# Twenty modulation products in attention: one accumulator row pair each, summed in two groups

## The chip, the cores and the metric

The kernel runs on one core of one Trainium2 chip. The metric is the device time of one execution in microseconds. The kernel before took 1193.83 us, the median of three runs (1192.38 to 1194.75).

## The reference, cut to what matters

Two layers act on 256 latent tokens and 256 context tokens of width 1024. Each layer has an attention part and a mixture-of-experts part, and both are modulated: shifts, scales and gates come from two conditioning vectors, `c` and `c_ctx`.

```
silu_c, silu_cc = silu(c), silu(c_ctx)
for l in range(2):
    sh1, sc1, g1, sh2, sc2, g2 = split(silu_c  @ ada_w[l] + ada_b[l], 6)   # ada_w[l]: 1024 x 6144
    (the same with silu_cc for the context tokens)
    h = rms(x) * (1 + sc1) + sh1
    y = attention(h, hc)                 # 16 query heads, 8 global and 8 local (window 128, with a sink)
    x = x + g1 * (y @ w_out[l])
    h = rms(x) * (1 + sc2) + sh2
    x = x + g2 * grouped_moe(h)          # 16 experts, the best 2 of each token
```

The modulation vectors are a product of a 2 x 1024 matrix with 2 x 6144 columns of weights, 50 MB in all. This case is about where these products are gathered.

## The kernel before, in words

Each engine has its own program, written out by hand in the order in which it runs, and semaphores tie the programs together. Everything is float32, so every TensorE product is issued as two passes, and a count of matmuls in the profile is twice the count of `mm` calls, except for transposes.

**Modulation units.** The 12288 columns of `ada_w` are cut into 24 units of 512 columns (2 MB each). `ada_unit` (lines 349 to 367) multiplies one unit on TensorE: `scv`, 128 x 2 per k-block, is the stationary operand and the 512 weight columns are moving. Eight k-blocks go to four column groups of the array, k and k + 4 to the same one, so that the result lies in bank 7 as four partial sums, at rows 32q and 32q + 1. ScalarE copies the whole bank to `parts` in `h_t` (`ada_parts`, line 763), TensorE transposes it in four blocks of 128 x 128 into bank 2 or 7 (`ada_turn`, line 376), and VectorE adds the four partial sums into `mods` (`ada_sum`, line 963). A unit may write bank 7 only when the sum of the unit before it is done (line 360). Units 0 to 3 run before layer 0's projections. Units 4 to 23 run inside layer 0's attention.

**Attention** (TensorE from line 437, ScalarE from 765, VectorE from 994). Layer 0 has 64 steps, one for each query head and tile of 128 tokens, called heads here. Heads 0 to 31 have 512 keys and heads 32 to 63 have 256. Of each 16 heads the last eight are local; those of the first 32 have a mask product added (line 467). TensorE works in iterations of two heads n and n + 1: the scores of both (464, 467), the transposes of the probabilities of heads n - 3 and n - 2 (476), in every second iteration the value products of four heads (493), and last a modulation unit, if one is due. A unit is due where a head number is 1 modulo 3, its `ada_turn` where it is 0 modulo 3, between the two transposes; so of three iterations two have a unit and one has none. VectorE does for head n the row maximum (1006, 1008 or 1011), then for head n - 1 the reciprocal and the scaling of the probabilities (1020, 1021). ScalarE does the exponential of head n (777, 778) and copies the transposed probabilities of head n - 2 (789), then `ada_parts` where n is 1 modulo 3.

**The weight loads.** SP issues the loads (`load_ada`, line 263) in one queue. In attention four slots of `ring` hold the units; a slot is loaded again when the unit that used it has signalled `ada_used`. Behind unit 23's load stand the two halves of `w_out`, gated by units 20 and 21, and behind them expert weights, gated by unit 23, by the end of attention and by the end of the output projection. Loads 5 to 7 are issued when the projections are done and two small transfers of swapped keys have landed.

**After attention** come the output projection (line 523), the norm, the routing and a loop over experts, all on TensorE's path. The expert weights are loaded slot by slot as the loop frees them.

Of the kernel before, what the change touches and what calls it, by code (L numbers as in the profile page):

```python
# [49 lines left out]
MAX_CHUNKS = [n * NE + 2 * t * P // CHUNK for n, t in zip(LEAST, TOK_TILES)]  # L50
ROWS = P * -(-CHUNK * (max(MAX_CHUNKS) + 1) // P)
GT = max(MAX_CHUNKS) + 2

C_ID, C_BLK, C_SWP = 0, P, 2 * P
# [52 lines left out]
def backbone(nc, x, c, ctx_in, c_ctx, ada_w, ada_b, attn_norm_g, ffn_norm_g, w_in, qn_global, kn_global,  # L108
             qn_local, kn_local, sink_logit, w_out, router_w, router_b, w_gate, w_up, w_down, table, out):
    with ExitStack() as stack:  # L110
# [3 lines left out]
        def sem(name):  # L114
            return stack.enter_context(nc.semaphore(name))
# [50 lines left out]
        rope_b = probs[:, 1, 0:SEQ]  # L166
        probs_t = h_t[:, 0:4, :]
        parts = h_t[:, 5, :]
        y_t = tokm[:, :, :].rearrange("p t n -> p (t n)").rearrange("p (k n) -> p k n", k=KD)
        smx = h_t[:, 4, 0:64]  # L170
        negmax = h_t[:, 4, 64:128]
# [48 lines left out]
        yg_in = [[sem(f"yg_in{l}_{t}") for t in range(4)] for l in range(DEPTH)]  # L220
        y_scaled, y_summed, c_turned, xc_ready = sem("y_scaled"), sem("y_summed"), sem("c_turned"), sem("xc_ready")
        o_turned, o_act, o_dve, out_done = sem("o_turned"), sem("o_act"), sem("o_dve"), sem("out_done")
        dve_step = sem("dve_step")

        def ada_bank(u):

            return bank[2 if u < 4 else 7]

        def units(l):

# [115 lines left out]
        def _(pe):  # L346
# [3 lines left out]
            def ada_unit(u):  # L350

                if u < 4:
                    s = (6, 0, 1, 2)[u]
                    pe.wait_ge(ada_in[u], 16)
                else:
                    s = (6, 3, 4, 5)[u % 4]
                    pe.wait_ge(ada2_in[u % 4], 16 * (u // 4))
                if u > 3:
                    pe.wait_ge(ada_summed, u)  # L360
                elif u > 0:
                    pe.wait_ge(parts_ready, u)
                w = ring[:, s, :].rearrange("p (k n) -> p k n", k=KD)
                for k in range(KD):
                    q = k % 4
                    last = mm(bank[7][32 * q:32 * q + 2, :], scv[:, k, :], w[:, k, :],  # L366
                              start=(k < 4), stop=(k >= 4))
                last.then_inc(ada_used, 1)

            def ada_turn(u):  # L370

                pe.wait_ge(parts_ready, u + 1)
                if 0 < u < 4:
                    pe.wait_ge(ada_summed, u)
                for m in range(4):
                    last = turn(ada_bank(u)[:, P * m:P * m + P], parts[:, P * m:P * m + P], ident)
                last.then_inc(ada_turned, 1)

            def first_sums():
# [58 lines left out]
            def attention(l):  # L438
                ub, gb = sum(UNITS[:l]), sum(UNITS[:l]) // 4
                us = units(l)  # L440

                def scores(n):
                    tt, T = us[n][0:2]
                    k0, kn = keys(tt)
                    if n == 0:
                        pe.wait_ge(qk_done, 10 * (l + 1))
                        pe.wait_ge(swapped, 64 * (l + 1))
                    if n >= 4:
                        pe.wait_ge(exp_done, ub + n - 2)

                    parts, masked = [(0, kn)], None
                    if T == 1 and tt < 2:
                        masked = (P, 2 * P) if tt == 0 else (0, P)
                        parts = [(0, P), (2 * P, kn), masked] if tt == 0 else [(P, kn), masked]
                    pair = []
                    for i in (n, n + 1):
                        kv, r = us[i][2:4]
                        a = r % 2
                        rows = slice(HD * a, HD * a + HD)
                        pair.append(((qk_t[:, T] if a == kv else sq[T])[rows, k0:k0 + kn],  # L460
                                     qk_t[rows, 2 + 4 * T + 2 * kv + r // 2, P * tt:P * tt + P], bank[i % 4]))
                    for c0, c1 in parts:
                        for k_t, q_t, o in pair:
                            last = mm(o[:, c0:c1], q_t, k_t[:, c0:c1], start=True, stop=(c0, c1) != masked)  # L464
                    if masked:
                        for k_t, q_t, o in pair:
                            last = mm(o[:, masked[0]:masked[1]], ident, band[tt], start=False, stop=True)
                    last.then_inc(sc_done, 2)

                def turn_probs(n):  # L470
                    tt = us[n][0]
                    pe.wait_ge(p_scaled, ub + n + 1)
                    if n >= 2:
                        pe.wait_ge(pt_ready, ub + n - 1)
                    for q in range(keys(tt)[1] // P):
                        last = turn(bank[4 + n % 2][:, P * q:P * q + P], probs[:, n % 4, P * q:P * q + P], ident)  # L476
                    last.then_inc(p_turned, 1)

                def values(g):

                    tt, T, kv, _ = us[4 * g]
                    k0, kn = keys(tt)
                    pe.wait_ge(pt_ready, ub + 4 * g + 4)
                    if g == 0:
                        pe.wait_ge(v_ready, 2 * (l + 1))
                    if g >= 1:
                        pe.wait_ge(y_evac, gb + g)
                    nk = kn // P
                    col = P * T + HD * kv  # L490
                    for q in range(nk):
                        for odd in range(2):
                            last = mm(bank[6][HD * odd:HD * odd + HD, 0:256],  # L493
                                      v_tok[:, k0 // P + q, col:col + HD],
                                      probs_t[:, q, 256 * odd:256 * odd + 256], start=(q == 0), stop=(q == nk - 1))
                    last.then_inc(pv_done, 1)

                for n in range(0, UNITS[l] + 4, 2):
                    if n < UNITS[l]:
                        scores(n)  # L500
                    if 3 <= n < UNITS[l] + 3:
                        turn_probs(n - 3)
                    for i in (n, n + 1):
                        if l == 0 and i % 3 == 0 and 0 < i <= 60:
                            ada_turn(3 + i // 3)
                    if 2 <= n < UNITS[l] + 2:
                        turn_probs(n - 2)
                    if n >= 6 and n % 4 == 2:
                        values(n // 4 - 1)
                    for i in (n, n + 1):  # L510
                        if l == 0 and i % 3 == 1 and i < 60:
                            ada_unit(4 + i // 3)
# [180 lines left out]
        def _(act):  # L693
# [62 lines left out]
                    do(v_tok[:, 2 * q:2 * q + 2, :].rearrange("p t n -> p (t n)"), bank[5 + q][:, :],  # L756
                       ACT.Identity).then_inc(v_ready, 1)

            def ada_parts(u):
                act.wait_ge(ada_used, u + 1)  # L760
                if u > 0:
                    act.wait_ge(ada_turned, u)
                do(parts, bank[7][:, :], ACT.Identity).then_inc(parts_ready, 1)

            def attention(l):
# [26 lines left out]
                for n in range(UNITS[l] + 2):  # L792
                    if n < UNITS[l]:
                        exponentials(n)
                    if n >= 2:
                        probs_out(n - 2)
                    if l == 0 and n % 3 == 1 and n // 3 < 20:
                        ada_parts(4 + n // 3)

            def route(l):  # L800
                nt = TOK_TILES[l]
# [138 lines left out]
        def _(dve):  # L940
# [3 lines left out]
            def link(ins):  # L944

                chain[0] += 1
                ins.then_inc(dve_step, 1)
                dve.wait_ge(dve_step, chain[0])
# [7 lines left out]
                    gv = vec[:, g0:g0 + KD].unsqueeze(2).to_broadcast([P, KD, 2])  # L956
                    link(v.tensor_tensor(gain[:, l, w], gain[:, l, w], gv, ALU.mult))

            def ada_sum(u):

                dve.wait_ge(ada_turned, u + 1)
                ps = ada_bank(u)[:, :].rearrange("p (m q x) -> p m x q", m=4, q=4)[:, :, 0:2, :]
                v.tensor_reduce(mods[:, 4 * u:4 * u + 4, :], ps, AX.X, ALU.add).then_inc(ada_summed, 1)

            def add_bias(m0, m1):
                dve.wait_ge(ada_summed, m1 // 4)
                bias = vec[:, V_ADAB + m0:V_ADAB + m1].unsqueeze(2).to_broadcast([P, m1 - m0, 2])
                link(v.tensor_tensor(mods[:, m0:m1, :], mods[:, m0:m1, :], bias, ALU.add))

# [25 lines left out]
            def attention(l):  # L995
# [2 lines left out]
                nu = UNITS[l]  # L998
                dve.wait_ge(v_mm, 2 * (l + 1))
                link(v.memset(esink[:, 0:nu], 0.0))  # L1000

                def maxima(n):
                    tt, T, kv, r = us[n]
# [27 lines left out]
                for n in range(nu + 4):  # L1031
                    if n < nu:
                        maxima(n)
                    if 1 <= n < nu + 1:
                        scale_probs(n - 1)
                    if n >= 7 and n % 4 == 3:
                        y_out(n // 4 - 1)
                    if l == 0 and n % 3 == 0 and 0 < n <= 60:
                        ada_sum(3 + n // 3)

            def add_attention(l):
                width = P * TOK_TILES[l]
# [246 lines left out]
```

## Time and profile before

| what | before |
|---|---|
| median of three runs | 1193.83 us |
| lowest and highest run | 1192.38 and 1194.75 us |
| span of the profiled execution | 1192.8 us |
| its engines: TensorE, weight loads, VectorE, ScalarE busy | 82%, 52%, 37%, 32% of the span |
| DMA, mean over the span | 254 GB/s |
| first score product of layer 0's attention | 147.96 us |
| first product of layer 0's output projection | 293.93 us |
| TensorE on the chain that ended last | 67% of the span |

The profiled execution is reported by its span, from its first to its last instruction; it has no time of its own beside that. The median of the runs is 1.0 us above this span, which is what lies around it.
### The profile page before, as it was taken

The numbers are of one execution on the slowest core, as the hardware profiler recorded it, in microseconds if no ns is written. First come the engines' busy times: TensorE is split into PE (matmuls) and PEld (weight loads), VectorE is DVE, ScalarE is ACT, GpSimd is POOL, SyncE is SP. The second block draws the span as 40 slices with busy tenths as digits, with TensorE's granted clock in tenths as the row PEclk, the third lists the DMA queues.
The fourth block names the chain that finished last, engine by engine and source line by source line (L and its number), as shares of the span: only waits on it lengthen the run. The fifth ranks groups of instructions, "written<-read, shape, count | busy, mean of one in ns | idle before, by whom it ended". The sixth has DMA issues, their size and how long they took to land.

```text
span 1192.8 us, 26429 instructions
## 1 busy us (share of the span) xinstructions
PE 980.8 (82%) x10601; PEld 623.3 (52%) x10602; DVE 435.6 (37%) x1194; ACT 380.8 (32%) x898; POOL 53.4 (4%) x96
## 2 busy tenths in 40 slices
PE   5699999888977999999999947998895855557982
PEld 2244654533437566767766625785584522324652
DVE  1356565666135222222222217568715200111222
ACT  3322265554014122222222224227703311322441
POOL 1000000000000000000000030000000000000001
PEclk9899999999995999999999977999996977877995
DMA  8993098798321089996989866005033899999933
GB/s 307 401 370 127 19 382 326 279 347 303 127 87 54 19 327 369 329 361 243 375 315 394 344 249 243 0 19 212 2 141 141 322 396 396 396 393 394 398 145 115
DMA packets 123776, 303.17 MB, mean 254 GB/s; under 512 B 5696, under 2 KB 5968, under 8 KB 123728
## 3 DMA queue, kind: packets, MB, share of 16 engines
q1 hardware_dynamic: 115872, 285.49, 64.2%
q0 software_dynamic: 6144, 16.79, 4.3%
q8 instruction: 33, 0.54, 0.2%
q10 hardware_dynamic: 1712, 0.23, 0.1%
q14 instruction: 15, 0.12, 0.0%
HBM read 290.95 MB, written 19.40 MB: 260 GB/s over the span
## 4 chain that ended last, share of the span: by engine, by line
PE 67%; SPq 10%; DVE 8%; DMA 7%; issue 4%; ACT 3%; ACTq 1%; POOL 1%; POOLq 0%; DVEq 0%
PE bank L577 17%; PE bank L423 10%; SPq L280 9%; PE bank L589 8%; PE bank L565 7%; PE bank L523 7%; PE bank L493 3%; PE bank L366 3%; PE bank L464 2%; DMA ring<-in_ada_w_dram 2%; DMA ring<-in_w_up_dram 2%; PE bank L476 2%; PE bank L534 1%; PE bank L432 1%; DVE h_t L1006 1%
## 5 line engine op out<-in xcount | busy, mean ns | idle before, releaser
L577 PE MATMUL bank<-ring,h_t 128*32 128x256 f32 x4160 | 257.0, 401 | 78.2 <-DMA ring<-in_w_up_dram 61.4
L577 PEld LDWEIGHTS bank<-ring,h_t 128*32 128x32 f32 x4160 | 162.7, 116 | 166.6 <-issue 108.4
L823 ACT COPY h_t<-bank 32x256 f32 x260 | 94.9, 365 | 223.6 <-PE bank L589 145.6
L1173 DVE TENSOR_TENSOR h_t<-h_t,bank 128x128 f32<-128x128 f32 x65 | 18.7, 288 | 324.9 <-ACT h_t L816 324.9
L589 PE MATMUL bank<-ring,h_t 128*32 128x256 f32 x2080 | 125.8, 380 | 7.7 <-issue 5.3
L423 PE MATMUL bank<-h_t,ring 128*128 128x512 f32 (+1 forms) x320 | 117.6, 522 | 12.3 <-ACT h_t L729 12.3
L565 PE MATMUL bank<-tokm,h_t 128*32 128x256 f32 x1760 | 111.3, 386 | 9.5 <-DVE h_t L1158 9.5
L589 PEld LDWEIGHTS bank<-ring,h_t 128*32 128x32 f32 x2080 | 77.8, 110 | 47.2 <-issue 17.8
L423 PEld LDWEIGHTS bank<-h_t,ring 128*128 128x128 f32 x320 | 62.4, 196 | 60.3 <-issue 40.9
L565 PEld LDWEIGHTS bank<-tokm,h_t 128*32 128x32 f32 x1760 | 67.9, 111 | 38.0 <-issue 11.2
L523 PE MATMUL bank<-tokm,ring 128*128 128x512 f32 (+1 forms) x256 | 83.1, 486 | 1.0 <-DVE tokm L1028 1.0
L816 ACT ACTIVATE h_t<-bank 128x128 f32<-128x128 f32 x65 | 18.1, 278 | 190.2 <-PE bank L577 190.2
L987 DVE RECIPROCAL work<-work 128x512 f32<-128x512 f32 (+1 forms) x20 | 54.3, 2713 | 58.7 <-ACT work L739 58.7
L1006 DVE TENSOR_REDUCE h_t<-bank 128x1 f32<-128x512 f32 (+1 forms) x96 | 57.4, 598 | 48.3 <-PE bank L464 26.9
L926 POOL DMA_DIRECT2D y_rows<-h_t x66 | 32.5, 493 | 888.3 <-ACT h_t L823 885.8
L789 ACT ACTIVATE h_t<-bank 128x512 f32<-128x512 f32 (+1 forms) x96 | 50.2, 524 | 57.3 <-PE bank L476 30.1
L523 PEld LDWEIGHTS bank<-tokm,ring 128*128 128x128 f32 x256 | 48.5, 190 | 35.7 <-issue 30.1
L778 ACT ACTIVATE ring<-bank,h_t 128x512 f32<-128x512 f32 (+1 forms) x96 | 58.6, 610 | 5.5 <-DVE h_t L1011 4.7
L476 PE MATMUL bank<-cst,ring 128*128 128x128 f32 x320 | 50.6, 280 | 8.0 <-DVE ring L1021 6.7
L1163 DVE STREAM_TRANSPOSE h_t<-bank 128x256 f32<-128x256 f32 x67 | 30.2, 450 | 53.4 <-PE bank L565 53.4
L476 PEld LDWEIGHTS bank<-cst,ring 128*128 128x128 f32 x320 | 35.3, 141 | 27.3 <-DVE ring L1021 19.6
L464 PE MATMUL bank<-ring 64*128 64x128 f32 (+3 forms) x144 | 47.0, 434 | 1.8 <-DMA work<-ring 1.8
(148 smaller groups left out, 994.9 us busy)
## 6 DMA issues: line engine op xcount, KB each, us to landing
ring<-in_w_gate_dram SPq DMA_DIRECT2D x32, 2048.0 KB, 12.7
ring<-in_w_up_dram SPq DMA_DIRECT2D x32, 2048.0 KB, 15.8
ring<-in_w_down_dram SPq DMA_DIRECT2D x32, 2048.0 KB, 16.4
ring<-in_ada_w_dram SPq DMA_DIRECT2D x24, 2048.0 KB, 11.0
ring<-in_w_in_dram SPq DMA_DIRECT2D x8, 1536.0 KB, 17.1
y_rows<-in_table_dram SPq DMA_DIRECT2D x1, 8704.0 KB, 45.7
y_rows<-h_t POOLq DMA_DIRECT2D x66, 128.0 KB, 5.2
ring<-in_w_out_dram SPq DMA_DIRECT2D x4, 2048.0 KB, 9.2
```

The costliest lines, as they stand in the source:

```text
L280: sp.dma_start(slot(s, k), src).then_inc(ew_in[l][s], 16)
L423: last = mm(bank[1 + i % 2][:, 0:widths[i]], qk_weights(i, k), h_t[:, k, 0:widths[i]], start=(k == 0), stop=(k == KD - 1))
L464: last = mm(o[:, c0:c1], q_t, k_t[:, c0:c1], start=True, stop=(c0, c1) != masked)
L476: last = turn(bank[4 + n % 2][:, P * q:P * q + P], probs[:, n % 4, P * q:P * q + P], ident)
L523: last = mm(bank[4 + m % 2][:, 0:P * nt], wout[k // 4][:, k % 4, P * m:P * m + P], y_t[:, k, 0:P * nt], start=(k == 0), stop=(k == KD - 1))
L565: last = mm(bank[5][CHUNK * q:CHUNK * q + CHUNK, 0:256], picks[:, tt, :], tokm[:, tt, 256 * q:256 * q + 256], start=(tt == 0), stop=(tt == ...
L577: last = mm(o.rearrange("r (s c i) -> r s c i", s=2, c=KF), hc_t[:, k, :], w[:, :, k, :, CHUNK * q:CHUNK * q + CHUNK], start=(k == 0), sto ...
L589: last = mm(bank[4][CHUNK * q:CHUNK * q + CHUNK, 0:256], he_t[:, k, :], wd[:, k, 256 * q:256 * q + 256], start=(k == 0), stop=(k == KF - 1))
L778: do(probs[:, n % 4, 0:kn], bank[n % 4][:, 0:kn], ACT.Exp, bias=negmax[:, n:n + 1], scale=SCALE, accum_out=lsum[:, n:n + 1]).then_inc(exp_ ...
L823: last = nc.scalar.copy(yrow[:, bass.ds(g % 2 * D + 256 * q, 256)], bank[4][CHUNK * q:CHUNK * q + CHUNK, 0:256])
L987: v.reciprocal(rstd[:, 0:n], rstd[:, 0:n])
L1006: link(v.tensor_reduce(smx[:, n:n + 1], bank[n % 4][:, 0:keys(tt)[1]], AX.X, ALU.max))
```

## The change: what it does

Units 4 to 23 are gathered in two groups, units 4 to 11 and 12 to 23. Each unit of a group adds into bank 7 at rows of its own: the stationary operand is now 32 columns wide, a window into `scv_wide` in which all but two columns are zero, and the place of the two columns is that of the unit within its group. The copy, the four transposes and the sum are made once for a group. They stand at head 22 (copy), 24 (transposes) and 25 (sum) for the first group, and at 58, 60 and 61 for the second. A unit waits for a sum only where it is the first of its group. `scv_wide` is set by a memset of 128 x 496 and a copy on VectorE at the start of layer 0's attention. Units 0 to 3 stay as they are.

```diff
+ADA_GROUPS = [(0, 1), (1, 2), (2, 3), (3, 4), (4, 12), (12, 24)]
+        scv_wide = h_t[:, 6, 0:496].rearrange("p (k c) -> p k c", k=KD)
             def ada_unit(u):
-                if u > 3:
-                    pe.wait_ge(ada_summed, u)
-                elif u > 0:
-                    pe.wait_ge(parts_ready, u)
+                n = [u0 <= u < u1 for u0, u1 in ADA_GROUPS].index(True)
+                u0, u1 = ADA_GROUPS[n]
+                if u == u0 and n > 3:
+                    pe.wait_ge(ada_summed, n)
+                    pe.wait_ge(scv_spaced, 1)
+                elif u == u0 and n > 0:
+                    pe.wait_ge(parts_ready, n)
...
+                        first_col = 30 - 2 * (u - u0)
+                        last = mm(bank[7][32 * q:32 * q + 32, :], scv_wide[:, k, first_col:first_col + 32], w[:, k, :],
+                                  start=(u == u0 and k < 4), stop=(u == u1 - 1 and k >= 4))
...
-                        if l == 0 and i % 3 == 0 and 0 < i <= 60:
-                            ada_turn(3 + i // 3)
+                        if l == 0 and i in (24, 60):
+                            ada_turn(4 if i == 24 else 5)
...
-                    if l == 0 and n % 3 == 1 and n // 3 < 20:
-                        ada_parts(4 + n // 3)
+                    if l == 0 and n in (22, 58):
+                        ada_parts(4 if n == 22 else 5)
...
+                ps = ada_bank(n)[:, :].rearrange("p (m q j x) -> p m j x q", m=4, q=4, x=2)
+                sums = mods[:, 4 * u0:4 * u1, :].rearrange("p (j m) x -> p m j x", m=4)
+                for m in range(4):
+                    last = v.tensor_reduce(sums[:, m], ps[:, m, 0:u1 - u0], AX.X, ALU.add)
+                last.then_inc(ada_summed, 1)
...
+                if l == 0:
+                    link(v.memset(scv_wide, 0.0))
+                    v.tensor_copy(scv_wide[:, :, 30:32], scv[:, :, :]).then_inc(scv_spaced, 1)
...
-                    if l == 0 and n % 3 == 0 and 0 < n <= 60:
-                        ada_sum(3 + n // 3)
+                    if l == 0 and n in (25, 61):
+                        ada_sum(4 if n == 25 else 5)
```

## Rows read from the trace of the kernel before

**Rows 1.** Windows by stretch: length, engines' busy time (count), granted clock, DMA share, GB/s.
```profile
157.76:229.97 72.21, 65.80 (x530) 37.14 (x532) 42.48 (x135) 41.52 (x105) 0.00 (x0) 1.00 0.91 333
229.97:284.55 54.58, 47.56 (x364) 21.44 (x366) 33.78 (x140) 30.27 (x102) 0.00 (x0) 1.00 0.85 310
284.55:293.93 9.38, 6.41 (x42) 3.31 (x42) 6.17 (x27) 6.26 (x23) 0.00 (x0) 1.00 0.89 324
804.60:868.60 64.00, 56.44 (x401) 35.29 (x401) 49.37 (x153) 45.59 (x114) 0.00 (x0) 0.97 0.26 99
```

**Rows 2.** Waits of TensorE from 157 to 285 us: total us, times, longest.
```profile
PE bank L376 <- ACT h_t L763: 9.7, 9, 1.2
PE bank L366 <- DVE mods L963: 2.2, 4, 0.7
```

**Rows 3.** Chain of waits in the heads with 512 keys: start, length, what.
```profile
162.10 1.83 PE bank L366 x16
...
166.61 0.60 ACT h_t L763
167.26 0.66 PE bank L376 x4
167.91 0.44 PE bank L476 x4
...
170.54 0.61 ACT h_t L789
171.19 1.95 PE bank L493 x16
...
174.97 1.08 PE bank L464 x12
176.04 0.66 PE bank L467 x4
...
190.81 1.06 PE bank L464 x4
```

**Rows 4.** The same chain in the heads with 256 keys.
```profile
245.59 0.22 PE bank L476 x2
245.81 1.01 PE bank L493 x8
246.83 0.63 PE bank L464 x4
...
287.91 0.34 DVE h_t L1006
...
289.14 0.34 DVE h_t L1006
```

**Rows 5.** The same chain in layer 1's attention, where VectorE sets the pace.
```profile
825.75 0.70 DVE h_t L1006
...
827.48 0.61 DVE h_t L1006
```

**Rows 6.** Groups by form, 157.76 to 229.97 us: busy us, mean ns, idle before.
```profile
L366 PEld LDWEIGHTS bank<-ring,scv 128*2 128x2 f32 x144 | 2.9, 83 | 9.7 <-issue 9.7
L963 DVE TENSOR_REDUCE mods<-bank 128x8 f32<-128x32 f32 x9 | 1.6, 183 | 0.0
```

**Rows 7.** Chain of waits in layer 0's expert loop: 64 passes of 256 columns.
```profile
484.03 3.45 PE bank L577 x64
```

**Rows 8.** Groups by form in that expert loop, 384 to 690 us.
```profile
L577 PEld LDWEIGHTS bank<-ring,h_t 128*32 128x32 f32 x2688 | 101.7, 110 | 58.6 <-issue 17.1 <-DVE h_t L1163 2.5
```

**Rows 9.** VectorE at the start of attention, in order of time.
```profile
146.29 0.11 DVE L1000 MEMSET h_t<- 128x64 f32 x1 [3.25 <-PE bank L432]
...
149.19 0.69 DVE L1006 TENSOR_REDUCE h_t<-bank 128x1 f32<-128x512 f32 x1 [2.79 <-PE bank L464]
```

**Rows 10.** Chain of waits: the first unit load that attention waits for.
```profile
147.90 7.86 DMA ring<-in_ada_w_dram
```

**Rows 11.** Window where the loads ran without a pause: columns as in Rows 1.
```profile
240.00:280.00 40.00, 34.88 (x267) 15.38 (x265) 25.40 (x107) 22.89 (x81) 0.00 (x0) 1.00 1.00 367
```

More of the change, by code:

```diff
@@ L222, in backbone, with ada_bank @@
         o_turned, o_act, o_dve, out_done = sem("o_turned"), sem("o_act"), sem("o_dve"), sem("out_done")
+        scv_spaced = sem("scv_spaced")
         dve_step = sem("dve_step")
-        def ada_bank(u):
-            return bank[2 if u < 4 else 7]
+        def ada_bank(n):
+            return bank[2 if n < 4 else 7]
         def units(l):
@@ L365, in ada_unit, with ada_turn @@
                     q = k % 4
-                    last = mm(bank[7][32 * q:32 * q + 2, :], scv[:, k, :], w[:, k, :],
-                              start=(k < 4), stop=(k >= 4))
+                    if u < 4:
+                        last = mm(bank[7][32 * q:32 * q + 2, :], scv[:, k, :], w[:, k, :],
+                                  start=(k < 4), stop=(k >= 4))
+                    else:
+                        first_col = 30 - 2 * (u - u0)
+                        last = mm(bank[7][32 * q:32 * q + 32, :], scv_wide[:, k, first_col:first_col + 32], w[:, k, :],
+                                  start=(u == u0 and k < 4), stop=(u == u1 - 1 and k >= 4))
                 last.then_inc(ada_used, 1)
[L370 to L374, printed above, removed]
+            def ada_turn(n):
+                pe.wait_ge(parts_ready, n + 1)
+                if 0 < n < 4:
+                    pe.wait_ge(ada_summed, n)
                 for m in range(4):
-                    last = turn(ada_bank(u)[:, P * m:P * m + P], parts[:, P * m:P * m + P], ident)
+                    last = turn(ada_bank(n)[:, P * m:P * m + P], parts[:, P * m:P * m + P], ident)
                 last.then_inc(ada_turned, 1)
@@ L757, in qkv, with ada_parts @@
                        ACT.Identity).then_inc(v_ready, 1)
[L759 to L762, printed above, removed]
+            def ada_parts(n):
+                act.wait_ge(ada_used, ADA_GROUPS[n][1])
+                if n > 0:
+                    act.wait_ge(ada_turned, n)
                 do(parts, bank[7][:, :], ACT.Identity).then_inc(parts_ready, 1)
@@ L957, in gains, with ada_sum @@
                     link(v.tensor_tensor(gain[:, l, w], gain[:, l, w], gv, ALU.mult))
[L959 to L963, printed above, removed]
+            def ada_sum(n):
+                dve.wait_ge(ada_turned, n + 1)
+                u0, u1 = ADA_GROUPS[n]
+                ps = ada_bank(n)[:, :].rearrange("p (m q j x) -> p m j x q", m=4, q=4, x=2)
[3 more added lines that the diff above has]
+                last.then_inc(ada_summed, 1)
             def add_bias(m0, m1):
-                dve.wait_ge(ada_summed, m1 // 4)
+                dve.wait_ge(ada_summed, 4 if m1 == 2 * KD else len(ADA_GROUPS))
                 bias = vec[:, V_ADAB + m0:V_ADAB + m1].unsqueeze(2).to_broadcast([P, m1 - m0, 2])
```

## The prediction

> **What bounds the kernel now.** I read the page's chain first: TensorE holds most of it, so a change counts if it shortens TensorE's way through its stage. The stage here is layer 0's attention. The windows by stretch cut it where units end: from the end of unit 5 to that of unit 14 (27 heads, nearly all with 512 keys), to that of unit 23 (27 heads, nearly all with 256 keys), and a tail to the output projection [rows 1]. TensorE is busy 91% of the first and 87% of the second stretch, VectorE 59% and 62%, ScalarE 57% and 55%. So TensorE is near its bound and the rest is short waits. The table of waits names them: nine times TensorE stands before `ada_turn` for the copy of bank 7, 9.7 us in all, and four times a unit stands for the sum of the one before, 2.2 us [rows 2]. The chain in order of time shows one case: the copy 0.60, then the four transposes 0.66, where 0.44 is the price of four transposes in flow [rows 3]. The copy is late because unit and `ada_turn` are only scores and one transpose apart, and ScalarE, in order, has put everything behind the copy.
>
> **What is removed.** 20 sets of copy, transposes and sum become 2. The set of unit 4 lay before unit 5's load had landed, and unit 23's stays as the second group's. Of the 18 between, unit 11's is replaced by the first group's, so 17 leave TensorE's path: 17 x 0.44 = 7.5 us of transposes [rows 3]. With them go the waits, 9.7 + 2.2 = 11.9 us [rows 2], and the slower start after a wait, 9 x (0.66 - 0.44) = 2.0 us. Ceiling: 21.4 us. The waits don't all go, because the heads have waits of their own which these have covered. I therefore build both stretches anew.
>
> **First stretch, 72.2 us now.** A pair of heads costs 1.06 without a mask, 1.08 + 0.66 = 1.74 with one, on average 0.70 a head; transposes 0.44 a head; value products 1.95 for four heads, 0.49 a head [rows 3]. That is 1.63 x 27 = 44.0 us, and nine units of 1.83 are 16.5: work of 60.5 us. New waits: value products wait for the copy of their last transposes, 0.61 with 0.44 of the next transposes beside it, so 0.2 seven times, 1.4 us. VectorE takes 1.73 for a masked head [rows 5], so two heads need 3.46; TensorE, in an iteration with neither unit nor values, comes back after 0.88 + 1.74 + 0.44 = 3.06. That happens once in 12 heads, 0.4 each, 0.9 us. Sum 62.8 us.
>
> **The switch of groups**, in the same stretch. Unit 12 now waits for the sum at VectorE's head 25, which stands behind two heads' work, not one: from the end of scores(24), 2 x 1.73, then the sum, then 0.14 to start, 4.2 us. TensorE has 3 x 0.44 = 1.3 to do until then, so it stands 2.9 us. Behind the waiting unit stand scores(26) and all the rest of TensorE; VectorE and ScalarE run dry behind them. With the group's transposes, 3.3 us. The four reductions take 32 elements in 183 ns now [rows 6], and 512 in 690 ns [rows 9]; 64 or 96 elements lie near the lower end, I take 0.2 each, 0.7 for four (0.7 to 2.8). First stretch: 66.1 us, a saving of 6.1.
>
> **Second stretch, 54.6 us now.** Scores 0.63 a pair, transposes 0.22 a head, values 1.01 for four [rows 4]: 0.79 x 27 = 21.3 us; nine units 16.5; the three heads of the larger size that reach into it 1.5. Work of 39.3 us. VectorE's pace is 1.24 a head [rows 4], 2.48 for two, against TensorE's 0.44 + 0.63 + 0.22 = 1.29: 1.2 once in 12 heads, 2.7 us. Waits before values I take at 0.35, seven times, 2.4 us. Sum 44.4 us, a saving of 10.2.
>
> **What is added.** (1) The memset and copy on VectorE. A memset of 64 columns took 0.11 us; 496 columns lie between that and 0.9 (8 times as much). VectorE is idle for 2.79 us just there, waiting for the first scores, which themselves wait for the swapped keys [rows 9]: nothing on the path; without that cover at most 1.0 us. (2) Stationary operands of 32 columns instead of 2. A load takes 110 ns in the expert loop against 83 [rows 6, 8]. The expert loop has the same shape of work: 64 passes of 256 columns on 32-column stationaries took 3.45 us, 54 ns a pass, so the loads lie beside the products and four passes run side by side [rows 7]. Sixteen passes of 512 columns at that rate are 1.72, against the 1.83 of a unit now. I charge only the first load of each unit, 20 x 0.027 = 0.5 us; bounds 0 and all 320 loads, 8.6 us. (3) In the tail VectorE is the chain [rows 4], and the second group's four reductions stand in it: 0.7 instead of 0.18, 0.5 us (bounds 0.5 and 2.6).
>
> Here a rule speaks against the change. The Trainium skill, "TensorE: Matmul & The Clock Gate", section "The mechanism" under Part 3, says that weight loads overlap running products only when the row group differs; here all products use all 128 rows. Rows 7 and 8 disagree: 64 loads of 110 ns are 7.0 us and the whole took 3.45. By the rule the sum would lose about 8 us; by the trace 0.5.
>
> **The loads' queue.** Each load is still freed by its own unit, so a faster loop asks earlier. A load of 2.1 MB at 367 GB/s takes 5.7 us [rows 11]; from issue to use the first took 7.9 [rows 10]. New pace: 7.3 us a unit in the first stretch, 4.9 in the second, so from unit 15 on the loads are slower than the loop and live on the lead of four slots. Unit 13 ends near 217, load 17 lands near 225, then each 5.7 later, load 23 near 259. Unit 23 starts near 267. The halves of `w_out` land near 265 and 271 and the projection starts near 279. Lead left: 7 us; the loads stay hidden. Unit 6 is tight as well: its load lands near 161.5 and it would now start at 161.6.
>
> **Sum.** 6.1 + 10.2 - 0.5 - 0.5 = 15.3 us. The gated expert loads (unit 23, end of attention, end of projection) all move with the stage, and the projection is 55 us of TensorE during which two pairs of them land, so I carry the whole 15.3 us through. The profiled span of 1192.8 becomes 1177.5; with the 1.0 us that lies around it, and from the median, 1178.5 us.
>
> **Rivals.**
> A. The heads' own latency takes the place of the removed waits. For: in layer 1, with no units at all, 32 heads take 64.0 us [rows 1] where TensorE's work is 1.63 x 32 = 52; a VectorE head costs 1.73. Against: a unit fills 1.83 us in two of three iterations. Then only the transposes go, 7.5, less the switch 2.9, less 1.0: 3.6, 1190.2 us.
> B. The loads run out. For: 100% DMA share from 240 to 280 already [rows 11]. Against: the lead of 7 us. If a load takes 6.7 beside denser traffic, the last units and `w_out` lose the lead and some 5 us: 1183.5 us.
> C. The weight loads of 32 columns are not hidden: 320 x 27 ns = 8.6 less the 0.5 charged, so 7.2 is left: 1186.6 us. This is what the Trainium skill's rule would give. Against it stand rows 7 and 8.
> D. Slower than before: the wide stationaries lose the running side by side of four column groups. A unit would be 16 passes of 213 ns (512 columns at the granted clock of 1.00), 3.4 us instead of 1.83, 20 times, +32 us: 1210 us. It decides from a pass rate of 155 ns on, where 15.3 us are used up. Rows 7 show 54 ns at 256 columns, so it would need a cause in the windows into `scv_wide` or in adding across units.
> E. It doesn't do what it says in time: the stage ends earlier, but the expert loop is bound by something that doesn't move. Against: every gate in SP's queue moves. 1193.8 us.
>
> **How the numbers follow.** Forecast 1173.5 to 1184, chance 0.60; A 0.15, B 0.10, C 0.05, D 0.05, E 0.05. What a measurement of this kernel tells from no change is about 0.2%, 2.4 us. Faster: the forecast, A, B, C, 0.90; same: E, 0.05; slower: D, 0.05. The range starts at 1173 (the ceiling of 21.4 us, less little) and reaches to 1189.5, into the better part of A, and leaves out D, E and the rest of A, about 0.2.
>
> **What would show it.** The four transposes appear six times in the trace, 24 instead of 96. The first stretch takes 66 us, the second 44, the tail 10, and the projection starts at 279 us. Before unit 12 TensorE waits some 3 us for the sum. A unit's chain piece stays near 1.85. The waits for `ada_turn` fall from 9.7 to about 2. In the second stretch new waits before transposes (for VectorE) and values (for ScalarE) appear, about 5 us. No unit waits for its load beyond unit 6. I am wrong if the second stretch stays above 50 us (A), if units wait for loads (B), if a unit's piece grows by 0.3 or more (C, D), or if the stage gains and the end doesn't (E).

## The result and the profile after

The changed kernel took 1228.1 us, the median of four runs (1218.3 to 1233.7), against 1194.3 for the kernel before beside it: a ratio of 1.0269, 95% interval 1.0210 to 1.0328. It is 34 us slower where 15 us faster were forecast, and its runs scatter over 15 us where those of the kernel before stay within 3.1. The profiled execution is the fastest of the four, with a span of 1216.4 us.

The windows of the changed kernel by stretch; the first three answer to the first three of [rows 1], the others are discussed below.

```profile
157.22:223.97 66.75, 62.37 (x499) 34.61 (x498) 41.55 (x131) 36.98 (x97) 0.00 (x0) 1.00 0.99 360
223.97:270.87 46.90, 43.59 (x329) 18.41 (x328) 31.69 (x131) 25.89 (x93) 0.00 (x0) 1.00 0.97 361
270.87:280.87 10.00, 6.54 (x43) 3.36 (x43) 6.74 (x30) 6.26 (x23) 0.00 (x0) 1.00 0.90 334
464.10:475.00 10.90, 1.25 (x13) 0.38 (x14) 0.97 (x3) 1.46 (x4) 0.49 (x1) 0.69 0.97 354
475.00:480.00 5.00, 5.00 (x64) 2.97 (x63) 0.00 (x0) 0.00 (x0) 0.00 (x0) 0.64 0.03 12
```

The stage did nearly what was forecast: 66.8 us (forecast 66.1), 46.9 (44.4) and 10.0 (9.9). The output projection starts at 280.87 us, 13.1 us earlier than before. So everything was lost, and 23.6 us more, behind the stage that the change touches. Four marks and the end place the loss:

| TensorE reaches | before | after | difference |
|---|---|---|---|
| output projection | 293.93 | 280.87 | -13.1 |
| layer 0's expert loop | 387.04 | 374.86 | -12.2 |
| layer 0's combine | 713.12 | 737.18 | +24.1 |
| layer 1's expert loop | 919.79 | 943.45 | +23.7 |
| end of the span | 1192.8 | 1216.4 | +23.6 |

All of it lies in layer 0's expert loop, 326.1 us before and 362.3 after, though its code and its work are the same. The chain of waits in that loop, first of the kernel before at its first jump back, then of the changed kernel at the same jump:

```profile
474.11 1.73 PE bank L589 x32
475.84 1.07 issue
476.91 3.66 PE bank L577 x64
```

```profile
462.39 1.73 PE bank L602 x32
464.12 6.99 issue
471.11 1.07 PE bank L590 x6
472.19 2.66 issue
474.84 5.23 PE bank L590 x57
```

"Issue" is idle time in which the engine waited for no other engine and no data transfer that the profile shows. It is 1.07 us in one and 6.99 + 2.66 in the other. The loop runs five times, so it has four jumps back, and the profiled execution has such a stop at three of them, at 464, 533 and 611 us. The granted clock falls to 0.50 during each stop and stays there for 3.7, 5.8 and 4.0 us behind it; that is the 0.64 in the window from 475 to 480, where 64 passes take 5.23 us instead of 3.66. The waits of TensorE in the loop and the page's row of the instruction queue, first of the kernel before, then of the changed one:

```profile
PE bank L577 <- issue: 10.3, 15, 1.1
q8 instruction: 33, 0.54, 0.2%
```

```profile
PE bank L590 <- issue: 36.0, 17, 7.3
q8 instruction: 60, 0.98, 0.3%
```

### The profile page after: what moved, and what is told of

Its sections match the earlier page's. It is cut to its first block, busy times and chain, and to the rows that moved or that the text cites. A ratio compares the mean times of both kernels' runs of the same rounds, so it can differ in the third digit from the quotient of the medians.

```text
span 1216.4 us, 26232 instructions
## 1 busy us (share of the span) xinstructions
PE 982.3 (81%) x10529; PEld 616.5 (51%) x10530; DVE 434.3 (36%) x1196; ACT 371.5 (31%) x880; POOL 53.2 (4%) x96
## 4 chain that ended last, share of the span: by engine, by line
PE 65%; SPq 10%; DVE 8%; DMA 7%; issue 6%; ACT 3%; ACTq 1%; POOL 1%; POOLq 0%; DVEq 0%
PE bank L590 17%; PE bank L436 9%; SPq L285 9%; PE bank L602 8%; PE bank L578 7%; PE bank L536 7%; PE bank L506 3%; PE bank L379 3%; DMA ring<-in_ada_w_dram 2%; PE bank L477 2%; DMA ring<-in_w_up_dram 2%; PE bank L489 2%; PE bank L547 1%; DVE h_t L1026 1%; PE bank L445 1%
## 5 line engine op out<-in xcount | busy, mean ns | idle before, releaser
L590 PE MATMUL bank<-ring,h_t 128*32 128x256 f32 x4160 | 269.1, 410 | 104.1 <-DMA ring<-in_w_up_dram 61.2
L590 PEld LDWEIGHTS bank<-ring,h_t 128*32 128x32 f32 x4160 | 165.6, 118 | 200.1 <-issue 142.5
L602 PE MATMUL bank<-ring,h_t 128*32 128x256 f32 x2080 | 129.9, 381 | 7.7 <-issue 5.3
L578 PE MATMUL bank<-tokm,h_t 128*32 128x256 f32 x1760 | 114.9, 386 | 9.5 <-DVE h_t L1178 9.5
L602 PEld LDWEIGHTS bank<-ring,h_t 128*32 128x32 f32 x2080 | 78.9, 110 | 48.0 <-issue 17.8
L489 PE MATMUL bank<-cst,ring 128*128 128x128 f32 x320 | 49.0, 281 | 11.8 <-DVE ring L1041 10.5
## 6 DMA issues: line engine op xcount, KB each, us to landing
ring<-in_w_gate_dram SPq DMA_DIRECT2D x32, 2048.0 KB, 12.8
ring<-in_ada_w_dram SPq DMA_DIRECT2D x24, 2048.0 KB, 12.9
y_rows<-in_table_dram SPq DMA_DIRECT2D x1, 8704.0 KB, 47.6
```

Of the source, the lines that this page charges most:

```text
L578: last = mm(bank[5][CHUNK * q:CHUNK * q + CHUNK, 0:256], picks[:, tt, :], tokm[:, tt, 256 * q:256 * q + 256], start=(tt == 0), stop=(tt == ...
L590: last = mm(o.rearrange("r (s c i) -> r s c i", s=2, c=KF), hc_t[:, k, :], w[:, :, k, :, CHUNK * q:CHUNK * q + CHUNK], start=(k == 0), sto ...
L602: last = mm(bank[4][CHUNK * q:CHUNK * q + CHUNK, 0:256], he_t[:, k, :], wd[:, k, 256 * q:256 * q + 256], start=(k == 0), stop=(k == KF - 1))
```

## The experiments

The fillers in all of them are waits on a semaphore that is already past its value, written in pairs; each pair is one instruction. In the changed kernel TensorE's first product starts at 12.8 us; 162 fillers at the start delay it to 18.8, and 81 hardly (13.0). They take about 0.11 us each, and until 12.8 us TensorE is idle in any case.

**1. The old place for the changed kernel.** 162 fillers.

```diff
+            for _ in range(324):
+                pe.wait_ge(down_mm[0], 1)
             pe.wait_ge(cst_in, 16)
```

> The changed kernel with 162 more instructions at the start of TensorE's program: waits that are already met, while TensorE stands idle for its first inputs. 162 is what the change took out of TensorE's program ahead of the expert loop, so the loop lies again where it lay before. Theory P (placement): layer 0's expert loop is TensorE's longest loop body, some 1600 instructions or 6.25 blocks of 16 KB, and whether it stays resident depends on where it starts within a block. Then the instruction queue shows about 33 packets again instead of 60, the three stops of 10 us at the jump back are gone, the loop takes 305 us instead of 341, and the attention's gain of 13 us stays: 1181 us. Theory D (dynamics: the loop starts earlier against its weight loads, or the wide stationaries leave something behind): still 1218 to 1233 us, 60 packets.

Measured: 1190.0 us (seven runs, 1188.4 to 1194.0), ratio 0.9951 (0.9938 to 0.9964). 33 packets, no stop above 1.1 us, loop 386.1 to 711.9. Everything of the change is still there; what differs is the place of the code, and a start that is later by 6.0 us. That counts against theory D, and experiments 3 and 4 settle it. The kernel is 38 us faster for 162 instructions that do nothing. It stays 9 us above the 1181 expected: the fillers held the start up by 6.0 us, which had not been counted, and by the output projection the delay against the changed kernel is 8.5 us (289.35 against 280.87).

**2. A new place, 81 fillers.** The same edit with 162 waits.

> The changed kernel with 81 instructions instead of 162. Theory P: the loop starts just over a block boundary, which is the best place it can have, 7 blocks; so fast as well, 1181 us, although no kernel so far had this place. Were it the old place itself that matters (what lies ahead of the loop, or the total length), 1218 us or more. Theory D: 1218 to 1233 us.

Measured: 1185.6 us (four runs, 1182.7 to 1187.8), ratio 0.9918 (0.9889 to 0.9948), 33 packets, 5 us above the 1181 expected. So it isn't the old place that counts but a class of places.

**3. One block later.** 256 fillers.

> The changed kernel with 256 more instructions, one block: the loop lies one whole block later and at the same place within it as in the changed kernel. Theory P: slow as the changed kernel, 1218 to 1233 us, about 60 packets. If more instructions ahead of the loop help by themselves, or the waits at the start change the timing, 1181 us.

Measured: 1243.9 us (1237.9 to 1251.3), ratio 1.0425 (1.0367 to 1.0484), 61 packets, three stops of 9.6 to 10.5 us. The start is held up by 16.4 us (first product at 29.2), about as much as the 15.8 us that the time lies above the changed kernel's. More instructions don't help, and a later start doesn't either; the place within a block decides.

**4. The kernel before, at the bad place.** 94 fillers in the kernel without the change.

> The kernel before, attention unchanged, with 94 instructions more at the start: its loop now lies at the place within a block where the changed kernel's lies. Theory P: the loop loses 25 to 50 us with nothing of the change in it, stops of about 10 us at the jump back, about 60 packets: 1230 to 1245 us. Theory D: 1194 us, since nothing is different but waits already met.

Measured: 1241.9 us (1235.0 to 1243.9), ratio 1.0381 (1.0337 to 1.0425). Its page and its chain:

```profile
q8 instruction: 70, 1.15, 0.4%
```

```profile
477.65 7.01 issue
...
485.73 2.65 issue
...
685.64 6.93 issue
```

This is the test from the other side: no part of the change is in this kernel, its attention is that of before (projection at 295.7), and it loses 46 us. It has the stop at all four jumps, where the profiled run of the changed kernel has it at three. The fillers of experiment 3 give the same place within a block and three stops, so the place doesn't fix the number; what does is open. That the changed kernel's other runs, up to 15 us slower, had the fourth stop too is not shown, as only one run is profiled.

**5. Fillers behind the loop.**

```diff
                 experts(l)
+                if l == 0:
+                    for _ in range(162):
+                        pe.wait_ge(down_mm[0], 1)
                 combine(l)
```

> The changed kernel with 81 fillers behind layer 0's expert loop, where TensorE waits for the gathered rows. The total length of TensorE's program and the place of everything behind are those of the version with 81 at the start, but the first loop lies where the changed kernel has it. Theory P: slow, 1218 to 1235 us, about 60 packets. If the total length or layer 1's place mattered: about 1186 us.

Measured: 1218.8 us (two runs, 1217.8 and 1219.8), ratio 1.0194, 60 packets, three stops. The time lies at the lower edge of the changed kernel's own, and 33 us above that of the same fillers at the start. The length of the program and the place of layer 1's code don't matter. Layer 1's loop (736 instructions) has its packets only in its first round, in the kernel before and in the changed one.

**6. and 7. Where the step lies.** 48 fillers (24 at the start, 12 each ahead of the waits for the routing mask and for the routing), and 24 fillers at the start.

> The changed kernel with 48 fillers ahead of layer 0's expert loop: 24 at the start and 12 each at the two waits of the routing, so that none of them is on TensorE's path. Theory P: what counts is whether the 1601 instructions of the loop touch 7 or 8 blocks of 256. The loaded program begins some instructions ahead of the one written; from the kernels so far that offset lies between 20 and 114. With 48 fillers the loop starts at 219 plus the offset, so it touches 7 blocks if the offset is 37 or more: then 33 packets, no stops, and as the fillers cost nothing 1181 to 1183 us. With an offset under 37, slow: about 1220 us.

> The changed kernel with 24 fillers at the start: the loop starts at 195 plus the offset. Theory P: fast (1183 us, 33 packets) if the offset is 61 or more, slow (1218 us or more, 60 packets) if it is less. Nothing between the two: it's a step and not a slope. If the time followed the number of fillers, it would lie between 1186 and 1218.

Measured: with 48, 1186.5 us (six runs, 1183.3 to 1188.5), ratio 0.9927 (0.9909 to 0.9946), 4 us above the 1181 to 1183 expected. With 24, 1242.2 us (two runs, 1241.2 and 1243.2), ratio 1.0395. Instruction queue and waits of the one with 48, then of the one with 24:

```profile
q8 instruction: 33, 0.54, 0.2%
PE bank L593 <- issue: 10.6, 15, 1.1
```

```profile
q8 instruction: 69, 1.13, 0.4%
PE bank L590 <- issue: 58.3, 15, 13.0
```

A step, as the theory says, between 24 and 48 fillers: the offset is 37 to 60 instructions. (The 114 in the first expectation above should be 84, since from 85 on the changed kernel's loop would touch seven blocks; nothing hangs on it.) Here all four stops are 12.9 to 13.0 us long, in one piece, and the kernel is slower than the changed one. The price of a stop thus depends on the place too.

**8. Place or size.** One token tile left out of the gathers of layer 0, and 48 fillers to keep the start.

```diff
-                    for tt in range(nt):
+                    used = nt - 1 if l == 0 else nt
+                    for tt in range(used):
```

> The changed kernel in which layer 0 gathers rows of three token tiles instead of four (the fourth tile's rows are left out), which takes 96 instructions out of the loop, and 48 fillers at the start, so that the loop starts exactly where the changed kernel's starts. Theory P: place and size count together. With 1505 instructions from the same start the loop touches 7 blocks instead of 8: no stops at the jump back, some 33 packets, though the start is the bad one. The work left out itself is worth some 30 us (0.43 us for each of 65 gathers). If the start's place alone counted: stops of 9.7 us as in the changed kernel.

Measured: 1164.0 us (two runs, 1162.3 and 1165.8), 32 packets, no stop above 1.1 us, the first jump included. The time can't be compared, since the kernel leaves work out; the stops and packets can. The loop starts where the changed kernel's starts and is 96 instructions shorter, which puts its end into the seventh block. So it isn't the start alone, nor how near to a block's end the jump lands: start and size count together, as the number of blocks touched would have it.

**9. and 10. What a stop costs.** Layer 0's expert weights loaded by half, then by a sixteenth.

```diff
+                    n = 4096 // k
+                    if l == 0:
+                        n = n // 2
-                    sp.dma_start(slot(s, k), src)...
+                    sp.dma_start(slot(s, k)[:, :, 0:n], src[:, :, 0:n])...
```

> The changed kernel with layer 0's expert weights loaded by half (half the columns of each slot; the rest of the slot holds older data, so layer 0's experts compute something else; the instructions, their order and places are the same). Theory P with its price: at each jump back TensorE waits for a block of instructions that stands behind the weight loads just issued, two of 2 MB, 10 us at 390 GB/s. With half the bytes the stops fall from some 9.7 us to about 5, the packets stay at about 60. If the price were a fixed cost of a jump to a block that isn't resident, the stops would stay near 9.7 us.

> The changed kernel with a sixteenth of layer 0's expert weights loaded (32 or 64 columns of each slot; the experts compute something else). With half the bytes the stops were 7.2 to 8.2 us instead of 9.7, so traffic is not the main price. If the rest is a fixed price of a block that isn't resident, the stops stay at 6 to 7.5 us with hardly any weight traffic. If it was still the queue ahead of the block, they fall under 3 us.

Measured stops at the four jumps, by half and by a sixteenth:

```profile
468.00 8.23 issue
...
536.12 8.11 issue
...
610.94 7.56 issue
...
669.90 7.23 issue
```

```profile
468.12 4.38 issue
...
531.29 4.94 issue
...
602.52 4.72 issue
...
660.05 4.88 issue
```

Neither theory had it. Against 9.7 us with full loads (mean of three, the two pieces added) the stops are 7.8 with half and 4.7 with a sixteenth, where DMA moved 33 GB/s from 500 to 560 us. So about 4.7 us are left with hardly any weight traffic, and 5 more come with it. Not in proportion: half the bytes take only 1.9 off. The time was 1216.3 and 1205.8 us (two runs each), both with 69 packets.

The starts of the instruction packets divide a stop further. With a sixteenth of the loads the first packet starts with the stop (468.0) and TensorE goes on 4.5 us later, though the packet itself takes 1.1. With full loads the first packet starts only 2.6 us after the stop began (466.7), and TensorE goes on 4.4 us behind its start, for 1.07 us; then it stands again, as the next block isn't there either: that packet starts 5.7 us after the first, against 3.2 with a sixteenth. With half the loads the first starts 3.6 us after the stop began and the second 3.3 later. So a stop holds two fetches one behind the other, and what weight traffic adds lies in the waits for their starts. With 24 fillers the first packet starts 2.8 us after the stop began, the second 6.1 later, and TensorE goes on only 4.1 behind the second, 12.9 in one piece. The counted place agrees: there the jump lands 1 to 24 instructions ahead of a block's end, in the changed kernel 25 to 48.

**11. The change with the place mended.** 35 fillers ahead of each of the two waits of layer 0's routing, none at the start.

> The changed kernel with 70 filler instructions (waits already met) ahead of layer 0's expert loop, 35 where TensorE waits for the routing mask and 35 where it waits for the routing, both times idle for 5 us or more. At 0.11 us each they cost nothing there. Theory P: the loop starts just past or at a block boundary, 33 packets, no long stops; the start of the kernel is not touched, so the whole 13 us of the attention stay: 1181 us against 1194. If the 1186 us of the version with 81 came from something other than its fillers at the start, 1184 to 1187.

Measured: 1186.1 us (six runs, 1183.7 to 1190.0), ratio 0.9927 (0.9906 to 0.9948). Its profiled execution keeps the stage's gain whole: projection at 281.20, loop at 376.56, combine at 702.79, end of the span at 1182.0 against 1192.8. Of the 12.7 us at the projection 10.8 arrive. The time is 5 us above the 1181 expected, as in the expectation's second case; one wait of TensorE shows the fillers themselves, which took longer than the idle time that was to hide them:

```profile
PE bank L566 <- issue: 2.8, 1, 2.8
```

**12. The sums one head earlier.**

```diff
-                    if l == 0 and n in (25, 61):
-                        ada_sum(4 if n == 25 else 5)
+                    if l == 0 and n in (24, 60):
+                        ada_sum(4 if n == 24 else 5)
```

> The same, and the sums of the two groups stand one head earlier on VectorE, at heads 24 and 60 instead of 25 and 61. TensorE stood 2.5 us before unit 12 for the sum. Theory: the sum is ready one head's work (1.6 us) earlier, TensorE stands about 0.9 us, and up to 1.6 us is gained: 1179.5 us. If the heads behind it make up for the wait in any case, equal to the version without it.

Measured: 1185.3 us (1182.7 to 1188.0), ratio 0.9910 (0.9891 to 0.9929). TensorE's wait before unit 12 fell from 2.52 to 0.89 us as expected. The stage takes 133.0 us from first scores to projection, against 133.6: part of the gain goes into other waits, and in the medians the two can't be told apart, where 1179.5 us had been expected. It has the lowest median of all kernels that do the whole work, by less than the measurement resolves.

## Why the prediction was wrong

**The stage, right.** The terms can be checked one by one in the changed kernel. The chain at the switch of groups:

```profile
202.81 0.44 PE bank L389 x4
203.24 0.44 PE bank L489 x4
203.68 2.52 issue
206.20 1.92 PE bank L379 x16
```

The wait was forecast at 2.9 and is 2.52. The waits of TensorE from 157 to 281 us, in the place of [rows 2]:

```profile
PE bank L489 <- DVE ring L1041: 5.0, 10, 0.8
PE bank L506 <- ACT h_t L802: 3.0, 11, 0.5
PE bank L379 <- issue: 2.5, 1, 2.5
```

The 11.9 us of waits are gone, and those of the heads' own are 8.0, as the argument had it. The second stretch came out 2.5 us longer than forecast, and not by its waits: they are 3.3 us there (2.0 for VectorE, 1.3 for ScalarE) where 5.1 were forecast. TensorE is busy for 43.6 us in it, and the sum had 39.3 of work. So the total came nearer than its terms, by luck. Row 2 of [rows 1] would have given the work: 47.6 us busy less nine sets of transposes at 0.44 are 43.6. No unit after unit 5 waits for its load. The memset and the copy on VectorE and the group's reductions:

```profile
146.10 0.47 DVE L1019 MEMSET h_t<- 128x496 f32 x1 [0.17 <-DVE h_t L1017]
146.61 0.18 DVE L1020 COPY h_t<-scv 128x16 f32<-128x16 f32 x1
148.70 0.69 DVE L1026 TENSOR_REDUCE h_t<-bank 128x1 f32<-128x512 f32 x1 [1.91 <-PE bank L477]
...
274.10 0.74 DVE L979 TENSOR_REDUCE mods<-bank 128x24 f32<-128x96 f32 x4
```

The memset (0.47, bounds 0.11 to 0.9) is hidden, with 1.91 us of idle time left; four reductions take 0.74 (forecast 0.7). A unit's piece on the chain is 1.85 to 1.92 with 32 columns against 1.83 to 1.90 with two, and its weight loads 109 ns each:

```profile
L379 PEld LDWEIGHTS bank<-ring,h_t 128*32 128x32 f32 x288 | 7.6, 109 | 18.5 <-issue 18.5
```

Rival C and the rule behind it fall: the loads are hidden. So does rival D; rivals A and B did not come about. D's price was too low as well: it took 213 ns for a pass of 512 columns that runs alone, but in the output projection before, where passes run one after another, 119 recorded ones take 51.34 us, 0.43 each, at a granted clock of 1.00.

**The step that failed** is in the sum: "all move with the stage, and the projection is 55 us of TensorE during which two pairs of them land, so I carry the whole 15.3 us through." The weight loads and their gates do move. What was not looked at is that the change also moves code. It takes 162 instructions out of TensorE's program ahead of its longest loop, and the loop's seven touched blocks become eight. The sum has no term for it, which puts it at nothing. It costs 36 us in the loop of the profiled execution, 25.7 of it more waiting; the other 10.5 fit the lower clock in and behind the stops, which was not taken apart further. Rival D gave the right sign and half the size (+16 us against +34) with a mechanism that isn't there, and E had the place and not the sign. The test for it stood in the trace of before: the row of the instruction queue with its 33 packets, none in the rounds after the first, said that the loop was resident, and the count of the program said that a shift of the loop by 162 instructions could make it touch one block more. (With the offset known since, it had room for 54 to 77 instructions one way and 114 to 137 the other.) What that costs, no row of before shows.

**What the change is worth** is 13.1 us at the end of its stage, and in the medians 8.9 us with the place mended (1195.0 to 1186.1). That is 6 us less than the 15.3 forecast: above the forecast's 1184, and inside the wider range that reaches to 1189.5. 1.9 us are lost in that kernel's trace between the projection and the end, with fillers that outlast their cover. The rest is not settled: in the other mended kernels attention starts 1 to 2 us later than in the changed one (6.5 with 162 fillers) and the stretch from projection to loop is about 3 us longer, and the medians of the best four lie within 1.2 us of each other.

## What to carry to other kernels

A change to an unrolled program moves all code behind it. Before forecasting one, count the instructions of each long loop on its engine and the blocks it touches, and read the instruction queue in the profile: packets in every round of a loop mean that it is fetched anew. If a kernel gets slower in a stage that wasn't touched, with "issue" stops at a loop's jump back, shift the loop by half a block of instructions that do nothing, in both kernels, before looking for another reason. (For this loop 64 of 256 places are bad by the count, so half a block leads out of them.) And compare two versions of a kernel only with the place of the loops made equal or good in both.

## What the runs showed of the hardware

- A loop of 1601 instructions on TensorE stayed resident where by the count it touches seven blocks of 16 KB, and was fetched anew after three or all four of its jumps back where it touches eight; one of 1505 from a start at which 1601 is slow stayed resident. The step is between 24 and 48 instructions of shift, and moves the kernel by 56 us.
- A jump back to a block that is not there costs 4.7 us with little DMA traffic, 7.8 and 9.7 with half and full weight traffic, and 12.9 at another place of the loop with full traffic. In the changed kernel, with full, half and a sixteenth of the loads, TensorE goes on 4.4 to 5.0 us after the start of the packet that the jump asks for.
- Behind each stop of the changed kernel TensorE's clock is at its lower level (0.50 granted) for 3.7 to 5.8 us more. With full traffic a stop costs 11 to 14 us in all, by the length of the loop: 45 us for four in the kernel before at the bad place, 57 for four with 24 fillers.
- A wait that is already met is not free on TensorE: about 0.11 us for each instruction of this kind at the start of the program.
